# Retention's value projection, two heads in one 512-column pass

## The chip, the cores and the metric

The kernel runs on one core of a Trainium2 chip. The metric is the time of one execution on the device in microseconds. All stages of the kernel run in one launch; weights come from the chip's memory.

## The reference, cut to what matters

Two transformer blocks follow each other on 1024 tokens of width 1024. The part that the change touches is retention in the first block: four heads, with keys and queries of 128 columns and values of 256.

```python
h = rmsnorm(x, pre_mix_norm)
q_r, k_r, v_r, g_r, ... = split(h @ w_in)        # widths 512, 512, 1024, 1024, ...
# per head, chunks n of 128 tokens:
qk      = (q_n @ k_n.T) * decay
o_n     = qk @ v_n + (q_n * qdec) @ s            # v_n: 128 x 256
s       = gamma**128 * s + (k_n * kdec).T @ v_n
ret     = silu(g_r) * groupnorm(o)
```

The rest of the two blocks (attention, gates, two large feed-forward parts) is the same in both kernels.

## The kernel before, in words

Every engine runs its own program, and the five programs are written from the same generators, so that each engine meets the pieces of work in the same order; what an engine needs from another it waits for on a semaphore. TensorE (PE) multiplies, ScalarE (ACT) and VectorE (DVE) empty PSUM and do the elementwise work, GpSimd (POOL) some of it, and SyncE (SP) issues the DMAs.

A product in full precision is made of three matmuls in a reduced format: each operand is split into a high and a low part, and `mm3` (L659 to L662) adds high x high, high x low and low x high. The split hidden state is `hhi`, `hlo` (features on partitions, tokens along the row). Weights come in pieces of 128 x 1024 numbers. SP fetches a piece into one of three raw buffers (`raw`, L2686) as soon as the low part of the piece three before it has been formed. ACT copies it to its high part (`whi`, L1192) and DVE subtracts (`wlo`, L1757) into one of five slots, once PE is through with the piece five before. This is asked for in program order by `Feed.done` (L152): when a piece is done, the pieces up to five behind it are split there and then on ACT and DVE.

Projections with features on partitions (q, k, the gates) use `half_product` (L664): per piece two halves of 512 tokens, each of 24 matmuls of 512 columns with a `yield` after 12. The value projection has tokens on partitions: `token_product` (L684) makes, for a tile of 128 tokens and one head, 24 matmuls of 256 columns, the hidden state stationary and the weights moving. Per head there are 8 tiles, and two pieces, which stay in their slots until the last tile. ACT copies each tile to `rv` (L1344). `wide_product` (L697) is the same with 512 columns and four pieces; the second block's value projection uses it.

`retention_order` (L360) sets the order. `proj(0)` runs alone. Then, for each head h, the main work (two gate pieces of head h, then q, k and v of head h+1; for head 3 the last three gates) is interleaved with the side work `retention(h)`. `interleave` (L215) gives one side step per `ratio` main steps: 1.2 for heads 0 to 2, 1.0 for head 3. A main step is 12 matmuls of 512 columns or one value tile. The side work has 20 steps: for each of eight chunks a step `rt` (L843, L845: scores and transposed keys) and a step `ro` (L851, L855, L861: output and state update), two empty steps, and two steps `rT` of transposes (L872). On DVE `rt` stands for the masked scores `ss` (L1930) and the scaled queries (L1937), `ro` for the state `rs` (L1943, L1946) and the statistics (L1953, L1955); the first empty step holds the normalisation (L1960), `rT` the product with the gate into `ret` (L1976). On ACT they stand for the scaled keys `kd` (L1374) and the copy of `ro` (L1379). A gate is emptied by ACT (tanh, L1356), POOL (L2564) and DVE (L1911, `rg`). PE waits for `ss` before each `ro`.

The lines that the steps below name: `Feed.ahead` and `done` L140 and L152, `fetch` L2682, `values_evac` L1339, `retention` on PE L834 and on DVE L1919, `lsig` L502, `swahi` L506.

Of the kernel before, what the change touches and what calls it, by code (L numbers as in the profile page):

```python
# [7 lines left out]
F32R = mybir.dt.float32r  # L8
# [5 lines left out]
T = 1024  # L14
D = 1024
NT = 8
# [47 lines left out]
class Tally:  # L64
# [24 lines left out]
    def ok(self, *name):  # L89
        if not self.building:  # L90
            return None, 1
        topic, count = self.value[name]
        return self.sem(topic), count
# [116 lines left out]
def run(gen):  # L210
    for _ in gen:
        pass
# [53 lines left out]
            next(side, None)  # L266


def token_major(feed, token_product, name, col, spec):
    ns = [feed.piece("T", name, col, 0), feed.piece("T", name, col, 4)]  # L270
    for t in range(NT):
        token_product(ns, t, spec)
        if t == 7:
            for n in ns:
                feed.done(n)
        yield


def token_wide(feed, wide_product, name, spec):
    ns = [feed.piece("V", name, k) for k in range(4)]  # L280
    for t in range(NT):
        wide_product(ns, t, spec)
        if t == 7:
            for n in ns:
                feed.done(n)
        yield
# [70 lines left out]
        yield from values(n)  # L357


def retention_order(feed, half_product, token_product, q, k, v, g, lgate, retention, gates_left):  # L360

    def proj(h):
        yield from feature_major(feed, half_product, "q_r", h, q(h))
        yield from feature_major(feed, half_product, "k_r", h, k(h))
        yield from token_major(feed, token_product, "v_r", 256 * h, v(h))

    def main(h):
        for m in range(2):
            yield from feature_major(feed, half_product, "g_r", 2 * h + m, g(h, m))
        if h < 3:  # L370
            yield from proj(h + 1)
        else:
            lgate()
            yield from gates_left()

    run(proj(0))
    for h in range(4):
        interleave(main(h), retention(h), 1.2 if h < 3 else 1.0)


ITEMS = [(t, Q) for t in range(4) for Q in range(2)]
# [55 lines left out]
def programs(nc, ctx, I, out, sg, cd, yd, xd, ud, fd):  # L437
# [9 lines left out]
    def bank_of(*group):  # L447
        return bank[tally.banks[group]]

    def free(*group):  # L450

        return tally.sem(f"free{tally.banks[group]}"), 1

    def at(name, kb, shape, dt=F32):
        return nc.alloc_sbuf_tensor_at(name, shape, dt, offset=base + int(kb * 1024))
# [35 lines left out]
    rq = [at(f"rq{i}", FO + 4 * i, [128, T]) for i in range(2)]  # L491
    rk = [at(f"rk{i}", FO + 8 + 4 * i, [128, T]) for i in range(2)]
    rv = [at(f"rv{i}", FO + 16 + 8 * i, [128, NT, 256]) for i in range(2)]
    rg = at("rg", FO + 32, [128, 2, T])
    ro = at("ro", FO + 40, [128, NT, 256])
    dect = at("dect", FO + 48, [128, 1028])
# [2 lines left out]
    kd = at("kd", FO + 55.03125, [128, 128])  # L499
    rq2 = at("rq2", FO + 72, [128, 128])  # L500
    tb = at("tb", FO + 72.5, [128, 128])
    lsig = [at(f"lsig{i}", FO + o, [128, T]) for i, o in enumerate((0, 8, 16, 20))]  # L502


    rethi = at("rethi", HO, [128, 8, T], F32R)
    swahi = [at(f"swahi{k}", FO + o, [128, T], F32R) for k, o in enumerate((4, 12, 24, 28))]  # L506
    retlo = at("retlo", XO, [128, 8, T], F32R)
    swalo = at("swalo", FO + 56, [128, 4, T], F32R)
    Z = at("Z", HO + 32, [128, 8, T])
# [145 lines left out]
    def tensor_program(e):  # L655
# [25 lines left out]
                feed.done(n)  # L681
            yield

        def token_product(ns, t, spec):  # L684
            group, hi, lo = spec
            P, free = ring.open(*group, t)
            if t == 0:
                e.wait_ge(*ok("wlo", ns[1]))
            if free:
                e.wait_ge(*free)  # L690
            for k in range(8):
                n, c = ns[k // 4], 256 * (k % 4)
                i = mm3(P[:, 0:256], hi[:, k, 128 * t:128 * t + 128], lo[:, k, 128 * t:128 * t + 128],
                        whi[n % SLOTS][:, c:c + 256], wlo[n % SLOTS][:, c:c + 256], k == 0, k == 7)
            i.then_inc(*ring.full(*group, t))

        def wide_product(ns, t, spec):  # L697
            group, hi, lo = spec
            P, free = ring.open(*group, t)
# [134 lines left out]
        def retention(h):  # L834
            i = h % 2
            qtmp = [rq2, tb]
            for n in range(8):
                c = slice(128 * n, 128 * n + 128)
                P, free = ring.open("rt", h, n)
                e.wait_ge(*free)  # L840
                if n == 0:
                    e.wait_ge(*ok("free", "v_r", h, 7))
                x = e.matmul(P[:, 0:128], rk[i][:, c], rq[i][:, c], start=True, stop=True)  # L843
                if n < 7:
                    x = e.transpose(P[:, 128:256], rk[i][:, c], ident[:, :])  # L845
                x.then_inc(*ring.full("rt", h, n))
                yield
                P, free = ring.open("ro", h, n)
                e.wait_ge(*free)
                e.wait_ge(*ok("ss", h, n))  # L850
                x = e.matmul(P[:, 0:256], ss[n % 2][:, :], rv[i][:, n, :], start=True, stop=n == 0)  # L851
                if n > 0:
                    e.wait_ge(*ok("qd", h, n))
                    e.wait_ge(*ok("free", "kv", h, n - 1))
                    x = e.matmul(P[:, 0:256], qtmp[n % 2][:, :], rs[(n - 1) % 2][:, :], start=False, stop=True)  # L855
                x.then_inc(*ring.full("ro", h, n))
                if n < 7:
                    P, free = ring.open("kv", h, n)
                    e.wait_ge(*free)
                    e.wait_ge(*ok("free", "rt", h, n))  # L860
                    e.matmul(P[:, 0:256], kd[:, :], rv[i][:, n, :], start=True, stop=True).then_inc(*ring.full("kv", h, n))  # L861
                yield
            yield
            yield
            for m in range(2):
                for q in range(2):
                    P, free = ring.open("rT", h, m, q)
                    e.wait_ge(*free)
                    if m == 0 and q == 0:
                        e.wait_ge(*ok("rn", h))  # L870
                    for j in range(4):
                        x = e.transpose(P[:, 128 * j:128 * j + 128], ro[:, 4 * q + j, 128 * m:128 * m + 128], ident[:, :])  # L872
                    x.then_inc(*ring.full("rT", h, m, q))
                yield

        retention_order(feed, half_product, token_product,
                        lambda h: (("q_r", h), hhi, hlo, None), lambda h: (("k_r", h), hhi, hlo, None),
                        lambda h: (("v_r", h), hhi, hlo), lambda h, m: (("g_r", h, m), hhi, hlo, None),
                        nothing, retention, lambda: gates(range(13, 16)))
        tally.alias(("retention",), ring.latest)  # L880

# [175 lines left out]
                yield from feature_major(feed, half_product, "k_2", m, (("k_2", m), yhi, ylo, None))  # L1057

        interleave(qk_products(), idle(14), 1.5)
        run(token_wide(feed, wide_product, "v_2", (("v_2",), yhi, ylo)))  # L1060
        tally.alias(("v2_end",), ring.latest)


# [123 lines left out]
    def scalar_program(e):  # L1187
# [148 lines left out]
        interleave(gates(range(13), sig, ("ht", 7)), swa_order(swa_scores, swa_values), 0.95)  # L1336


        def values_evac(h):  # L1339
            def evac(t):  # L1340
                e.wait_ge(*ok("full", "v_r", h, t))
                if t == 0 and h > 1:
                    e.wait_ge(*ok("full", "ro", h - 2, 7))
                e.activation(rv[h % 2][:, t, :], bank_of("v_r", h, t)[:, 0:256], ACT.Copy).then_inc(*free("v_r", h, t))  # L1344
            return evac

        def before(h):
# [320 lines left out]
        first_stack()  # L1668
        e.wait_ge(*ok("qm", 0, 1, 1))
        e.activation(QM[0][1][64:128, :], q2[64:128, 0, :], ACT.Copy).then_inc(*up("qx", 0))  # L1670
        run(token_wide(feed, token_product, "v_2", v2_evac))


        def pooled(g):
# [79 lines left out]
    def vector_program(e):  # L1754
# [621 lines left out]
        for j in range(2):  # L2376
# [4 lines left out]
            e.memset(QM[0][j][o:o + 64, :].bitcast(F32), 0.0).then_inc(*up("aux", 0, j, 1))  # L2381
            e.wait_ge(*ok("aux", 0, j, 1))
            e.memset(QM[0][j][o + 32:o + 34, :].bitcast(F32), 1.0).then_inc(*up("aux", 0, j, 2))
        run(token_wide(feed, token_product, "v_2", v2_low))


        def pooled(g):
# [293 lines left out]
    def sync_program(e):  # L2681
# [281 lines left out]
        e.wait_ge(*ok("cst", 1))  # L2963
        fetch_c(0)
        feed.cap = CAT
        run(token_wide(feed, nothing, "v_2", None))


        def duplicates(t):
# [91 lines left out]
def pack(inputs, descs):  # L3061
# [17 lines left out]
    for n, d in enumerate(descs):  # L3079
        w = cuts[d[1]]  # L3080
        if d[0] == "F":
            wp[n].reshape(128, 8, 128)[:] = w[:, 128 * d[2]:128 * d[2] + 128].reshape(8, 128, 128).transpose(1, 0, 2)
        elif d[0] == "T":
            wp[n].reshape(128, 4, 256)[:] = w[128 * d[3]:128 * d[3] + 512, d[2]:d[2] + 256].reshape(4, 128, 256).transpose(1, 0, 2)
        elif d[0] == "V":
            wp[n].reshape(128, 2, 512)[:] = w[256 * d[2]:256 * d[2] + 256].reshape(2, 128, 512).transpose(1, 0, 2)
        elif d[0] == "B":
            k, c = d[2] // 2, 512 * (d[2] % 2)
            wp[n].reshape(128, 2, 512)[:] = w[512 * d[3]:512 * d[3] + 512, c:c + 512].reshape(2, 2, 128, 512)[:, k].transpose(1, 0, 2)
        elif d[0] == "D":  # L3090
            wp[n] = w[128 * d[2]:128 * d[2] + 128]
        else:
            wp[n].reshape(128, 2, 4, 128)[:] = w[:, 256 * d[2]:256 * d[2] + 256].reshape(4, 128, 2, 128).transpose(1, 2, 0, 3)
# [35 lines left out]
```

## Time and profile before

| | |
|---|---|
| median of 3 runs | 2548.62 us (2547.71 to 2549.22) |
| the profiled execution | 2549.9 us, span 2548.0 us |
| PE busy | 2496.6 us, 98% of the span |
| DVE, ACT, POOL busy | 1510.3, 1069.4, 189.7 us |
| share of the chain that ended last | PE 90%, DVE 6%, ACT 2%, DMA 1% |
| mean granted clock of TensorE | 0.995 |

The span goes from the first to the last instruction of the profiled execution. A row of a timeline gives the start in microseconds from the span's start, the time it took in microseconds, the engine, the line, the operation, output and inputs by the program's names, the shape and the count of merged instructions; in brackets the engine's idle time just before it and what ended it. Durations of matmuls overlap, so the time that a run of them takes is read from the starts. A matmul of full-precision operands appears twice (x2), for its two passes.

### The profile page before, as it was taken

How to read it: one execution, taken by the hardware profiler on the slowest of the kernel's cores; microseconds unless marked ns; L12 is line 12 of the kernel's file. 1: busy time of each engine (PE TensorE's matmuls, PEld its weight loads, DVE VectorE, ACT ScalarE, POOL GpSimd, SP SyncE). 2: the span in 40 equal slices, each digit the busy share in tenths (PEclk: the TensorE clock that was granted, in tenths of full speed). 3: DMA queues.
4: the chain of work that ended last, by engine and by line, in shares of the span. 5: the costliest groups of instructions: out<-in, count | busy, mean ns of one | idle time of the engine just before them, and what ended most of it. 6: DMA issues, size and time to landing. Idle time of an engine off the chain costs nothing.

```text
span 2548.0 us, 30521 instructions
## 1 busy us (share of the span) xinstructions
PE 2496.6 (98%) x11808; PEld 2058.3 (81%) x11808; DVE 1510.3 (59%) x2211; ACT 1069.4 (42%) x1708; POOL 189.7 (7%) x173
## 2 busy tenths in 40 slices
PE   7999999999999999999999999999999999999998
PEld 6777888888888788888888887866787888888886
DVE  4345223223533786877664754358767677876668
ACT  4344322222322564444434543357526544444432
POOL 0000000000020300000000110145111000000000
PEclk9999999999999999999999999999999999999999
DMA  4121211101421466778865541101315577788554
GB/s 166 67 75 66 75 42 37 39 34 57 159 83 64 164 214 209 243 256 330 306 247 182 188 155 62 34 20 40 116 51 194 184 250 262 252 336 323 188 188 168
DMA packets 148304, 390.06 MB, mean 153 GB/s; under 512 B 15136, under 2 KB 15392, under 8 KB 148032
## 3 DMA queue, kind: packets, MB, share of 16 engines
q1 hardware_dynamic: 148160, 388.11, 43.6%
q8 instruction: 94, 1.54, 0.2%
q14 instruction: 50, 0.41, 0.0%
HBM read 284.17 MB, written 100.73 MB: 151 GB/s over the span
## 4 chain that ended last, share of the span: by engine, by line
PE 90%; DVE 6%; ACT 2%; DMA 1%; issue 1%; SPq 0%; POOL 0%; DVEq 0%; ACTq 0%
PE bank L660 28%; PE bank L662 27%; PE bank L661 27%; DVE PAl L2402 1%; PE bank L734 1%; DVE st L2397 1%; DVE wlo L1757 1%; PE bank L784 1%; PE bank L1119 1%; PE bank L851 1%; PE bank L861 0%; PE bank L855 0%; PE bank L819 0%; ACT PAh L1697 0%; ACT whi L1192 0%
## 5 line engine op out<-in xcount | busy, mean ns | idle before, releaser
L1757 DVE TENSOR_TENSOR wlo<-raw,whi 128x1024 fp32r<-128x1024 f32 x122 | 150.1, 1237 | 255.3 <-ACT whi L1192 254.5
L660 PE MATMUL bank<-hhi,whi 128*128 128x512 f32 x608 | 249.0, 409 | 1.7 <-DVE hlo L1782 1.7
L662 PE MATMUL bank<-hhi,wlo 128*128 128x512 f32 x608 | 238.6, 392 | 0.0
L661 PE MATMUL bank<-hlo,whi 128*128 128x512 f32 x608 | 238.3, 392 | 0.0
L1192 ACT ACTIVATE whi<-raw 128x1024 fp32r<-128x1024 f32 x122 | 127.6, 1053 | 113.5 <-PE bank L662 86.2
L1490 ACT ACTIVATE r<-r 128x512 f32<-128x512 f32 x96 | 60.7, 632 | 190.7 <-DVE r L2227 133.1
L660 PEld LDWEIGHTS bank<-hhi,whi 128*128 128x128 f32 x608 | 114.8, 189 | 29.4 <-issue 6.7
L662 PEld LDWEIGHTS bank<-hhi,wlo 128*128 128x128 f32 x608 | 114.6, 188 | 25.3
L661 PEld LDWEIGHTS bank<-hlo,whi 128*128 128x128 f32 x608 | 115.0, 189 | 22.3
L660 PE MATMUL bank<-yhi,whi 128*128 128x512 f32 x192 | 74.9, 390 | 0.0
L662 PE MATMUL bank<-yhi,wlo 128*128 128x512 f32 x192 | 74.7, 389 | 0.0
L661 PE MATMUL bank<-ylo,whi 128*128 128x512 f32 x192 | 74.7, 389 | 0.0
L660 PE MATMUL bank<-whi,hhi 128*128 128x256 f32 x256 | 74.2, 290 | 0.0
L662 PE MATMUL bank<-whi,hlo 128*128 128x256 f32 x256 | 72.4, 283 | 0.0
L661 PE MATMUL bank<-wlo,hhi 128*128 128x256 f32 x256 | 72.4, 283 | 0.0
L660 PE MATMUL bank<-uw0bh,uw0ah 128*128 128x512 f32 x176 | 68.6, 390 | 0.1
L660 PE MATMUL bank<-uw1bh,uw1ah 128*128 128x512 f32 x176 | 68.5, 389 | 0.0
L662 PE MATMUL bank<-uw0bh,uw0al 128*128 128x512 f32 x176 | 68.5, 389 | 0.0
L662 PE MATMUL bank<-uw1bh,uw1al 128*128 128x512 f32 x176 | 68.5, 389 | 0.0
L661 PE MATMUL bank<-uw0bl,uw0ah 128*128 128x512 f32 x176 | 68.5, 389 | 0.0
L661 PE MATMUL bank<-uw1bl,uw1ah 128*128 128x512 f32 x176 | 68.5, 389 | 0.0
L2592 POOL TENSOR_TENSOR accX<-accX,acc 128x1024 f32<-128x1024 f32 x8 | 20.1, 2514 | 597.0 <-DVE acc L2282 597.0
(457 smaller groups left out, 7079.2 us busy)
## 6 DMA issues: line engine op xcount, KB each, us to landing
raw<-wp_d SPq DMA_DIRECT2D x122, 512.0 KB, 3.6
ra<-ud_d SPq DMA_DIRECT2D x112, 512.0 KB, 4.5
rawp<-wp_d SPq DMA_DIRECT2D x32, 1024.0 KB, 5.8
ud_d<-us SPq DMA_DIRECT2D x128, 256.0 KB, 5.7
rbh<-wp_d SPq DMA_DIRECT2D x64, 512.0 KB, 6.1
ud_d<-f SPq DMA_DIRECT2D x96, 256.0 KB, 2.2
rbw<-wp_d SPq DMA_DIRECT2D x48, 512.0 KB, 3.6
rbx<-wp_d SPq DMA_DIRECT2D x32, 512.0 KB, 8.3
```

The source lines that it names most:

```text
L660: e.matmul(P, sh, mh, start=first, stop=False, skip_group_check=more)
L661: e.matmul(P, sh, ml, start=False, stop=False, skip_group_check=more)
L662: return e.matmul(P, sl, mh, start=False, stop=last, skip_group_check=more)
L734: i = e.transpose(P[:, 128 * j:128 * j + 128], src[:, 128 * k:128 * k + 128], ident[:, :])
L784: i = e.matmul(P[:, 256 * (m % 2) + j0:256 * (m % 2) + 256], qs[64 * g:64 * g + 64, m, 128 * n:128 * n + 128], ks[64 * g:64 * g + 64, 128 ...
L851: x = e.matmul(P[:, 0:256], ss[n % 2][:, :], rv[i][:, n, :], start=True, stop=n == 0)
L1119: x = e.transpose(P[:, 128 * ii:128 * ii + 128], Pu[u % 2][ii][:, 128 * k:128 * k + 128], ident[:, :])
L1192: e.activation(whi[n % SLOTS][:, :], raw[n % RAWS][:, :], ACT.Copy).then_inc(*up("whi", n))
L1490: e.activation(r[:, :], r[:, :], ACT.Relu).then_inc(*up("relu", tag, name, p))
L1757: e.tensor_tensor(out=wlo[n % SLOTS][:, :], in0=raw[n % RAWS][:, :], in1=whi[n % SLOTS][:, :].bitcast(F32), op=ALU.subtract).then_inc(*up( ...
L2397: e.tensor_reduce(st[:, m:m + 1], psum[:, b:b + w], AXIS.X, ALU.min).then_inc(*up("mn", u, ii))
L2402: e.tensor_tensor(out=PAl[n % 3][:, c], in0=bank_of("pt", n)[:, c], in1=PAh[n % 3][:, c].bitcast(F32), op=ALU.subtract).then_inc(*free("pt ...
```

## The change

Values of two heads are projected at once. `proj(h)` projects values only for even h, with `token_wide` and `wide_product` (512 columns, four pieces, tiles of two heads), so heads 0 and 1 get theirs before head 0's retention, heads 2 and 3 during head 1's. ACT copies each tile in two activations, to the buffers of the two heads. Head 2's values get a buffer of their own, `rv2`, in the region of the last head's result; head 3's go to head 0's buffer. The ratios of `interleave` become 0.8, 1.2, 0.8 and 1.0, because the main work of heads 0 and 2 has 16 steps now (24 before). Two of the buffers `lsig` and two of `swahi` change places within the freed regions. `token_major` and `token_product` go; `token_wide` takes a column offset.

```diff
-def token_major(feed, token_product, name, col, spec):
-    ns = [feed.piece("T", name, col, 0), feed.piece("T", name, col, 4)]
...
-def token_wide(feed, wide_product, name, spec):
-    ns = [feed.piece("V", name, k) for k in range(4)]
+def token_wide(feed, wide_product, name, col, spec):
+    ns = [feed.piece("V", name, k, col) for k in range(4)]
     for t in range(NT):
         wide_product(ns, t, spec)
         if t == 7:
             for n in ns:
                 feed.done(n)
         yield
...
     def proj(h):
         yield from feature_major(feed, half_product, "q_r", h, q(h))
         yield from feature_major(feed, half_product, "k_r", h, k(h))
-        yield from token_major(feed, token_product, "v_r", 256 * h, v(h))
+        if h % 2 == 0:
+            yield from token_wide(feed, wide_product, "v_r", 256 * h, v(h // 2))
...
-        interleave(main(h), retention(h), 1.2 if h < 3 else 1.0)
+        interleave(main(h), retention(h), (0.8, 1.2, 0.8, 1.0)[h])
...
+    rv2 = at("rv2", XO + 24, [128, NT, 256])
+
+    def rv_of(h):
+        return (rv[0], rv[1], rv2, rv[0])[h]
...
-    lsig = [at(f"lsig{i}", FO + o, [128, T]) for i, o in enumerate((0, 8, 16, 20))]
+    lsig = [at(f"lsig{i}", FO + o, [128, T]) for i, o in enumerate((0, 8, 24, 28))]
...
-    swahi = [at(f"swahi{k}", FO + o, [128, T], F32R) for k, o in enumerate((4, 12, 24, 28))]
+    swahi = [at(f"swahi{k}", FO + o, [128, T], F32R) for k, o in enumerate((4, 12, 16, 20))]
...
                 if n == 0:
-                    e.wait_ge(*ok("free", "v_r", h, 7))
+                    e.wait_ge(*ok("free", "v_r", h // 2, 7))
...
-                x = e.matmul(P[:, 0:256], ss[n % 2][:, :], rv[i][:, n, :], start=True, stop=n == 0)
+                x = e.matmul(P[:, 0:256], ss[n % 2][:, :], rv_of(h)[:, n, :], start=True, stop=n == 0)
...
-        def values_evac(h):
+        def values_evac(p):
             def evac(t):
-                e.wait_ge(*ok("full", "v_r", h, t))
-                if t == 0 and h > 1:
-                    e.wait_ge(*ok("full", "ro", h - 2, 7))
-                e.activation(rv[h % 2][:, t, :], bank_of("v_r", h, t)[:, 0:256], ACT.Copy).then_inc(*free("v_r", h, t))
+                e.wait_ge(*ok("full", "v_r", p, t))
+                if t == 0 and p:
+                    e.wait_ge(*ok("full", "ro", 0, 7))
+                    e.wait_ge(*ok("free", "O", 7, 1))
+                e.activation(rv_of(2 * p)[:, t, :], bank_of("v_r", p, t)[:, 0:256], ACT.Copy)
+                e.activation(rv_of(2 * p + 1)[:, t, :], bank_of("v_r", p, t)[:, 256:512], ACT.Copy).then_inc(*free("v_r", p, t))
             return evac
```

## Rows read from the trace of the kernel before

**Rows 1.** The page: the chain that ended last, shares by engine.
```profile
PE 90%; DVE 6%; ACT 2%; DMA 1%; issue 1%; SPq 0%; POOL 0%; DVEq 0%; ACTq 0%
```
**Rows 2.** Busy time (and instructions) of PE, PEld, DVE, ACT, POOL in the stretch of retention.
```profile
341.67:637.00 295.33, 293.96 (x1633) 256.87 (x1632) 93.79 (x229) 78.82 (x146) 11.76 (x19) 1.00 0.12 41
```
**Rows 3.** Timeline of PE: the first narrow value matmul; first and last of 24 wide ones.
```profile
310.07 0.28 PE L660 MATMUL bank<-whi,hhi 128*128 128x256 f32 x1
...
1634.64 0.39 PE L660 MATMUL bank<-whi,yhi 128*128 128x512 f32 x1
...
1639.85 0.39 PE L662 MATMUL bank<-whi,ylo 128*128 128x512 f32 x1
```
**Rows 4.** Timelines around the end of head 0's value projection, by engine.
```profile
333.11 0.40 PE L660 MATMUL bank<-hhi,whi 128*128 128x512 f32 x1
...
338.58 0.38 PE L843 MATMUL bank<-rq,rk 128*128 128x128 f32 x2
...
341.67 0.60 PE L851 MATMUL bank<-rv,ss 128*128 128x256 f32 x2
...
333.31 0.38 ACT L1344 ACTIVATE rv<-bank 128x256 f32<-128x256 f32 x1 [2.50 <-PE bank L662]
333.59 2.00 ACT L1192 ACTIVATE whi<-raw 128x1024 fp32r<-128x1024 f32 x2
...
334.67 2.36 DVE L1757 TENSOR_TENSOR wlo<-raw,whi 128x1024 fp32r<-128x1024 f32 x2 [21.60 <-ACT whi L1192]
...
335.93 1.46 SPq L2686 DMA_DIRECT2D raw<-wp_d  x2
```
**Rows 5.** Timelines of SP and ACT: fetches out of an idle queue.
```profile
1479.34 1.28 SPq L2686 DMA_DIRECT2D raw<-wp_d  x3
...
1482.77 1.06 ACT L1192 ACTIVATE whi<-raw 128x1024 fp32r<-128x1024 f32 x1 [3.77 <-DMA raw<-wp_d]
1484.79 1.06 ACT L1192 ACTIVATE whi<-raw 128x1024 fp32r<-128x1024 f32 x1 [0.96 <-DMA raw<-wp_d]
```
**Rows 6.** Timelines of DVE and PE: head 0, the second chunk.
```profile
347.44 1.21 DVE L1757 TENSOR_TENSOR wlo<-raw,whi 128x1024 fp32r<-128x1024 f32 x1
348.57 0.28 DVE L1930 TENSOR_TENSOR ss<-bank,dect 128x128 f32<-128x128 f32 x1
...
349.00 0.67 PE L851 MATMUL bank<-rv,ss 128*128 128x256 f32 x2 [0.46 <-DVE ss L1930]
```
**Rows 7.** Timelines of PE and DVE: from head 2 to head 3.
```profile
577.45 1.03 PE L872 MATMUL bank<-ident,ro 128*128 128x128 f32 x8
...
581.29 1.28 DVE L1976 TENSOR_TENSOR ret<-bank,rg 128x512 f32<-128x512 f32 x2
582.49 0.28 DVE L1930 TENSOR_TENSOR ss<-bank,dect 128x128 f32<-128x128 f32 x1
...
584.16 0.60 PE L851 MATMUL bank<-rv,ss 128*128 128x256 f32 x2
```
**Rows 8.** Timelines of PE and DVE: head 3, the third chunk.
```profile
594.94 0.38 PE L843 MATMUL bank<-rq,rk 128*128 128x128 f32 x2
...
598.03 0.60 PE L851 MATMUL bank<-rv,ss 128*128 128x256 f32 x2
...
595.47 0.29 DVE L1930 TENSOR_TENSOR ss<-bank,dect 128x128 f32<-128x128 f32 x1 [0.35 <-PE bank L845]
```
**Rows 9.** Timeline of PE: head 0, the seventh chunk, behind a value tile.
```profile
390.25 0.28 PE L662 MATMUL bank<-whi,hlo 128*128 128x256 f32 x1
390.52 0.67 PE L851 MATMUL bank<-rv,ss 128*128 128x256 f32 x2
```
**Rows 10.** Timeline of PE, then a stretch's busy times, granted clock (0.50), DMA.
```profile
273.65 0.63 PE L819 MATMUL bank<-ident,p 128*128 128x128 f32 x4 [1.80 <-DVE p L1879]
...
1927.65 0.50 PE L660 MATMUL bank<-zhi,whi 128*128 128x512 f32 x1 [3.50 <-DVE wlo L1757]
...
1928.13:1931.55 3.42, 3.42 (x10) 2.62 (x9) 2.27 (x4) 1.37 (x2) 0.90 (x1) 0.50 0.28 104
```

More of the change, by code:

```diff
@@ L266, in feature_major_start @@
             next(side, None)
-def token_major(feed, token_product, name, col, spec):
-    ns = [feed.piece("T", name, col, 0), feed.piece("T", name, col, 4)]
[L271 to L276, printed above, removed]
-def token_wide(feed, wide_product, name, spec):
-    ns = [feed.piece("V", name, k) for k in range(4)]
+def token_wide(feed, wide_product, name, col, spec):
+    ns = [feed.piece("V", name, k, col) for k in range(4)]
     for t in range(NT):
@@ L357, in swa_order, with retention_order @@
         yield from values(n)
-def retention_order(feed, half_product, token_product, q, k, v, g, lgate, retention, gates_left):
+def retention_order(feed, half_product, wide_product, q, k, v, g, lgate, retention, gates_left):
     def proj(h):
@@ L682, in half_product @@
             yield
[L684 to L695, printed above, removed]
         def wide_product(ns, t, spec):
@@ L860, in retention @@
                     e.wait_ge(*ok("free", "rt", h, n))
-                    e.matmul(P[:, 0:256], kd[:, :], rv[i][:, n, :], start=True, stop=True).then_inc(*ring.full("kv", h, n))
+                    e.matmul(P[:, 0:256], kd[:, :], rv_of(h)[:, n, :], start=True, stop=True).then_inc(*ring.full("kv", h, n))
                 yield
@@ L874, in retention @@
                 yield
-        retention_order(feed, half_product, token_product,
+        retention_order(feed, half_product, wide_product,
                         lambda h: (("q_r", h), hhi, hlo, None), lambda h: (("k_r", h), hhi, hlo, None),
-                        lambda h: (("v_r", h), hhi, hlo), lambda h, m: (("g_r", h, m), hhi, hlo, None),
+                        lambda p: (("v_r", p), hhi, hlo), lambda h, m: (("g_r", h, m), hhi, hlo, None),
                         nothing, retention, lambda: gates(range(13, 16)))
@@ L1059, in tensor_program @@
         interleave(qk_products(), idle(14), 1.5)
-        run(token_wide(feed, wide_product, "v_2", (("v_2",), yhi, ylo)))
+        run(token_wide(feed, wide_product, "v_2", 0, (("v_2",), yhi, ylo)))
         tally.alias(("v2_end",), ring.latest)
@@ L1670, in scalar_program @@
         e.activation(QM[0][1][64:128, :], q2[64:128, 0, :], ACT.Copy).then_inc(*up("qx", 0))
-        run(token_wide(feed, token_product, "v_2", v2_evac))
+        run(token_wide(feed, token_product, "v_2", 0, v2_evac))
         def pooled(g):
@@ L2383, in vector_program @@
             e.memset(QM[0][j][o + 32:o + 34, :].bitcast(F32), 1.0).then_inc(*up("aux", 0, j, 2))
-        run(token_wide(feed, token_product, "v_2", v2_low))
+        run(token_wide(feed, token_product, "v_2", 0, v2_low))
         def pooled(g):
@@ L2965, in sync_program @@
         feed.cap = CAT
-        run(token_wide(feed, nothing, "v_2", None))
+        run(token_wide(feed, nothing, "v_2", 0, None))
         def duplicates(t):
@@ L3082, in pack @@
             wp[n].reshape(128, 8, 128)[:] = w[:, 128 * d[2]:128 * d[2] + 128].reshape(8, 128, 128).transpose(1, 0, 2)
-        elif d[0] == "T":
-            wp[n].reshape(128, 4, 256)[:] = w[128 * d[3]:128 * d[3] + 512, d[2]:d[2] + 256].reshape(4, 128, 256).transpose(1, 0, 2)
         elif d[0] == "V":
-            wp[n].reshape(128, 2, 512)[:] = w[256 * d[2]:256 * d[2] + 256].reshape(2, 128, 512).transpose(1, 0, 2)
+            wp[n].reshape(128, 2, 512)[:] = w[256 * d[2]:256 * d[2] + 256, d[3]:d[3] + 512].reshape(2, 128, 512).transpose(1, 0, 2)
         elif d[0] == "B":
```

## The prediction

> **What bounds the kernel now.** I read the chain of waits first: it lies on TensorE (PE) for 90% of the span [rows 1], so a change counts by what it does to PE's own time and by the waits it puts in front of PE. Next the busy time by stretches: in the retention stage PE is busy 293.96 of 295.33 us [rows 2]. There is nearly no idle time to win there, but also any new wait of PE is paid in full. Then the timeline of PE, for the pitch from one matmul's start to the next one's: a printed duration (0.28 us for 256 columns, 0.39 for 512) holds the drain, which overlaps the next matmul, and the durations alone would promise 65 us (768 x 0.28 - 384 x 0.39) where the pitches give 5 [rows 3]. Last the rows of ScalarE (ACT), VectorE (DVE) and the DMA queue around the end of the value projection.
>
> I count from E, the instant at which PE starts what follows the last value tile, and take the profiled execution, 2549.9 us (span 2548.0 and 1.9 around it); it lies 1.3 above the median of the runs, 2548.6.
>
> **1. The width.** 768 matmuls of 256 columns go, 384 of 512 come. The 256-wide pitch is (333.11 - 310.07) / 192 = 0.1200 us, the 512-wide one (1639.85 - 1634.64) / 23 = 0.2265 [rows 3, 4]; the wide run has the form of the new one, hidden values stationary and a 512-wide moving operand. A pair becomes 0.0135 us cheaper: 384 x 0.0135 = **-5.2 us**. The bounds are the two rows' rounding, -4.7 to -5.6.
> The Trainium skill, page TensorE: Matmul & The Clock Gate, section Back-to-back issue gap, gives a warm gap of N/2.4 ns plus about 2.5 ns. By that a pair would save only 2.5 ns and the change 1.0 us instead of 5.2; this trace shows some 13 ns a matmul beyond its columns, at both widths, and the measurement decides.
>
> **2. The end of a wide projection.** This is the term that turns the sign. Four weight pieces instead of two are released together, after tile 7, and each release makes ACT form the high part of one more piece (`whi`) and DVE its low part (`wlo`). In the trace two are formed: the copy of tile 7 at E+0.20, `whi` at E+0.48 and 0.95 later, `wlo` 1.08 after its `whi`, the next 1.14 after that, and the queue sends for a new raw piece 0.04 us after the first `wlo` ends [rows 4]. With the change the tile's copy is two activations (0.28 more), so `whi` starts at E+0.76 and the three pieces whose raw data are there have `wlo` at 1.84, 2.98 and 4.12. The fourth has no raw data: there are three raw buffers, and its fetch waits for the first `wlo`, which ends at 3.06. Fetch to `whi` takes 3.43 us (1482.77 - 1479.34) [rows 5], so `whi` is at 6.53 and `wlo` at 7.61.
> Queued behind this fourth `wlo` on DVE is the first masked score block `ss` of the next head, and behind that stands PE, at the head's first `ro` product. After a projection without rest, as at head 0: `ss` 1.13 after the `wlo` starts and PE 0.43 after `ss` starts [rows 6], so PE goes on at E+9.17. It gets there by itself, with one main step (12 matmuls of a gate product) ahead of `rt0` and one behind (the new ratio), at 2.74 (half of 338.58 - 333.11) + 3.09 (341.67 - 338.58, `rt0` and a step) = E+5.83 [rows 4]. Wait: **3.3 us**. At head 2 the two `ret` products of head 1 stand between (1.20 us to `ss`), so PE goes on at 7.61 + 1.14 + 1.20 + 0.43 = E+10.38; head 3 of the trace has this very order, and there PE arrives at 584.16 - 577.45 = E+6.71 [rows 7]. Wait: **3.7 us**. In the trace neither place waits, since two pieces end 2.4 us earlier and need no fetch. Bounds: the same fetch for nothing late (the third rival below, 2.3 us for both) and a `whi` 5.1 us after the fetch, as for the second of the fetches issued together (1484.79) [rows 5], 10.3 for both; I take 7.0, the row of a first fetch out of an idle queue, which this one is.
>
> **3. The rhythm of heads 0 and 2.** These heads' main work loses the value tiles: 16 steps of 2.72 us for 20 retention steps, at ratio 0.8. Every fifth retention step follows the one before at once. Written out, the order doubles `rt2 ro2`, `ro4 rt5`, `rt7 ro7` and the last two transposes. `ro` after `rt` without a main step between waits for `ss`: `ss` starts 0.53 after `rt2` and PE could go on 0.43 later, at 0.96, where now `rt` itself costs 3.09 - 2.72 = 0.37 [rows 8, 6]. That is 0.59; for `rt7`, which lacks the transpose, I take the same; four times: **+2.3 us** (0.3 each at least, as `ss` needs `rt`'s end and its own 0.29 us; 0.8 at most with a late DVE). The wait of 0.62 at `ro1` (0.46 printed as idle and 0.16 behind the drain of the matmul before, 0.39 - 0.23) [rows 6], where a gate's product with `rg` and a `wlo` are ahead of `ss`, exists in heads 0 to 2. With one main step ahead of `rt1`, as in head 3, it goes in heads 0 and 2, but the same neighbours (the end of the second gate piece, `rt4`, one step of `q`, `ro4`) bring it back at `ro4`: 0. In head 1 it stays. A 0.15 us wait at `ro6` behind a value tile (0.27 for 0.12) [rows 9] goes three times: **-0.4**. The transposes need the normalised `ro`; its chain over ACT and DVE begins with the empty step and has two main steps, 5.4 us, to run in, where it had more: 0, at most +0.4.
>
> **4. At nothing.** Copies out of PSUM: 32 either way. Pieces: eight either way, so SP issues as many fetches; in this stage nothing else stands in its queue until the last gates, and POOL is not moved past. The fourth piece at the start of a wide projection is split when `q` is done; the 10.9 us of `k` cover it, and without them it would cost the 2.3 us of a `whi` and a `wlo`. The moved regions (`rv2`, `lsig`, `swahi`) wait for events tens of us back.
>
> Sum without the clock: -5.2 + 7.0 + 2.3 - 0.4 = **+3.7 us**.
>
> **5. The clock.** An idle time of 3.50 us before PE is followed by 3.42 us at half the granted clock (1.2 instead of 2.4 GHz); that costs half of it, 1.7 us; an idle time of 1.80 is followed by none [rows 10]. My two waits, as the trace would print them (0.16 less, for the drain), are 3.2 and 3.5 us: nearest to the first row, a little under it. Bounds 0 and 3.4 us; I take one of the two, **+1.7**. So 2549.9 + 3.7 + 1.7 = 2555.3, and 1.3 less on the median's scale: **2554.0 us**.
>
> **The rivals.**
> - *Both waits, clock held*: +3.7, 2552.3 us. For it: both waits lie under 3.50. Against it: by little.
> - *Both waits, clock halved twice*: +7.1, 2555.7. For it: the second wait equals the row that is followed by the slow clock.
> - *On the other side, the fourth piece is in time*: if its raw data are there 3.6 us after E, its `wlo` follows the third at 5.26. PE then goes on at 5.26 + 1.13 + 0.43 = E+6.82 and E+8.03, two waits of 1.0 and 1.3 with no clock loss: 2548.6 - 5.2 + 2.3 + 1.9 = 2547.6, not slower. For it: fetches in this stage normally go out tens of us ahead. Against it: three raw buffers and the order of the splits.
> - *Faster*: neither the splits nor the doubled steps reach PE: -5.2 - 0.4, 2543.0. Against it: both waits are program order on DVE and not a matter of speed.
> - *The width saves nothing much*: the change does not do what it says, because the 13 ns a matmul beyond its columns (0.1200 us against 256/2.4 ns, 0.2265 against 512/2.4) are a matter of the neighbours and not of the count. With 0 instead of -5.2 the forecast becomes 2559.2. Against it: the two long runs [rows 3]. The Trainium skill's page named in step 1 stands near this rival, and the trace does not agree with it.
> - *One more wait of some 3 us*, for instance a late piece ahead of the wide tiles: 2557.
>
> **How the numbers follow.** Forecast (one clock loss) 0.35, none 0.25, two 0.20, fourth piece in time 0.08, faster 0.04, no gain from the width 0.03, another wait 0.05. A measurement of this kernel can tell about 0.2%, 5.1 us, so the lines are 2543.5 and 2553.7. The forecast lies just behind the upper line; with about 1 us of spread in its terms I give two thirds of it to slower. Slower: two thirds of 0.35, nearly all of 0.20, 0.08, and a little of 0.25, together 0.54. Faster 0.04. The rest, 0.42, is the same. The range, 2550.0 to 2557.5, takes the three clock cases with their unknown terms (four doubled steps at 0.3, a landing a little late) and leaves out the two lower rivals (0.12) and the upper ends (about 0.06).
>
> **What the changed profile would show.** Right: value copies 5.44 us apart in the two projections; behind each a fourth `whi` some 6.5 us after E that waited for a DMA; PE's first `ro` product of heads 0 and 2 with 3 to 4 us idle before it, released by `ss`; 0.4 us idle at `ro2`, `ro4`, `ro7` of these heads; the granted clock at 0.5 for one 3.4 us stretch behind at least one of the two. Wrong: PE's idle before these `ro` products under 1.5 us, or a pitch of the wide tiles off 0.227 us, or a span that moves elsewhere than between 310 and 640 us.

## The result, and the profile after

The changed kernel takes 2555.6 us (median; 2552.4 to 2557.5) where the kernel before takes 2548.8 on the same chip: ratio 1.0026 [1.0016, 1.0036], slower by 6.8 us. Two more comparisons on another occasion gave 1.0029 [1.0020, 1.0038] and 1.0028 [1.0019, 1.0037]. The forecast was 2554.0 with 2550.0 to 2557.5 around it and "slower" as the likeliest sign; the nearest of its cases, by the number, is the one with two clock losses, 2555.7. One execution of the kernel before took 3751 us at a mean clock of 0.624 and is left out of all comparisons.

The profiled execution took 2552.65 us, with a span of 2550.9. First the chain that ended last, on the page, against [rows 1]:

```profile
PE 91%; DVE 6%; ACT 2%; issue 1%; DMA 1%; SPq 0%; POOL 0%; DVEq 0%; ACTq 0%
```

Shares of a whole span can't show 7 us. The stretch of the stage can; it is compared with [rows 2]. The other lines are the two long waits of PE and the 3.4 us behind each (columns: busy time and instructions of PE, PEld, DVE, ACT, POOL, then granted clock, DMA share, GB/s):

```profile
341.00:637.00 296.00, 285.76 (x1316) 236.78 (x1315) 95.28 (x231) 76.88 (x144) 11.76 (x19) 0.99 0.13 43
357.60:361.02 3.42, 0.00 (x1) 0.04 (x1) 1.52 (x2) 1.17 (x2) 0.00 (x0) 1.00 0.92 293
361.02:364.44 3.42, 3.42 (x15) 2.85 (x16) 1.54 (x4) 1.09 (x3) 0.62 (x1) 1.00 0.46 163
523.50:526.53 3.03, 0.00 (x1) 0.00 (x0) 2.25 (x3) 0.75 (x1) 0.00 (x0) 1.00 0.68 246
526.53:529.94 3.41, 2.89 (x7) 2.37 (x8) 0.38 (x2) 2.52 (x4) 0.62 (x1) 0.50 0.45 157
```

PE had 1.4 us without work in this stage before; now it has 10.2 (296.00 - 285.76), although it has less to do. The list of waits from 300 to 640 us names what it waits for (total, times, longest), in the kernel before and then in the changed one:

```profile
PE bank L851 <- DVE ss L1930: 1.4, 3, 0.5
```
```profile
PE bank L834 <- DVE ss L1915: 10.2, 9, 3.5
```

Nine waits for the masked scores in place of three: seven of 0.46 to 0.48 us and two of some 3.5. The timelines of PE, DVE, ACT and SP at the first long one (L1742 is the `wlo` of the forecast, L1175 its `whi`, L1915 `ss`):

```profile
308.11 0.39 PE L656 MATMUL bank<-whi,hhi 128*128 128x512 f32 x1
...
350.95 0.39 PE L656 MATMUL bank<-whi,hhi 128*128 128x512 f32 x1
...
351.63 0.39 PE L656 MATMUL bank<-hhi,whi 128*128 128x512 f32 x1
...
361.02 0.67 PE L834 MATMUL bank<-rv,ss 128*128 128x256 f32 x2 [3.42 <-DVE ss L1915]
...
353.46 3.50 DVE L1742 TENSOR_TENSOR wlo<-raw,whi 128x1024 fp32r<-128x1024 f32 x3 [42.35 <-ACT whi L1175]
359.32 1.23 DVE L1742 TENSOR_TENSOR wlo<-raw,whi 128x1024 fp32r<-128x1024 f32 x1 [2.36 <-ACT whi L1175]
360.58 0.29 DVE L1915 TENSOR_TENSOR ss<-bank,dect 128x128 f32<-128x128 f32 x1
...
358.23 1.06 ACT L1175 ACTIVATE whi<-raw 128x1024 fp32r<-128x1024 f32 x1 [2.91 <-DMA raw<-wp_d]
...
354.72 6.18 SPq L2671 DMA_DIRECT2D raw<-wp_d  x4
```

Read it from the bottom. SP sends for the fourth raw piece at 354.72, when the first of the three `wlo` is done; the data let ACT start `whi` at 358.23, 3.51 us later; DVE, idle for 2.36 us, forms `wlo` at 359.32, and only then, at 360.58, the `ss` that PE has wanted since 357.60. Nothing here is slow. DVE stands idle with `ss` next but one in its program.

The second place has the `ret` products between `wlo` and `ss`:

```profile
516.62 1.04 PE L855 MATMUL bank<-ident,ro 128*128 128x128 f32 x8
...
527.05 1.19 PE L834 MATMUL bank<-rv,ss 128*128 128x256 f32 x2 [3.55 <-DVE ss L1915]
...
523.19 1.06 ACT L1175 ACTIVATE whi<-raw 128x1024 fp32r<-128x1024 f32 x1 [2.87 <-DMA raw<-wp_d]
...
524.28 1.22 DVE L1742 TENSOR_TENSOR wlo<-raw,whi 128x1024 fp32r<-128x1024 f32 x1 [2.33 <-ACT whi L1175]
525.43 1.28 DVE L1961 TENSOR_TENSOR ret<-bank,rg 128x512 f32<-128x512 f32 x2
526.62 0.28 DVE L1915 TENSOR_TENSOR ss<-bank,dect 128x128 f32<-128x128 f32 x1
```

### The profile page after: what moved, and what is told of

Same layout as the page of the kernel before. It is cut to its first block, busy times and chain, and to the rows that moved or that the text cites. A ratio compares the mean times of both kernels' runs of the same rounds, so it can differ in the third digit from the quotient of the medians.

```text
span 2550.9 us, 29750 instructions
## 1 busy us (share of the span) xinstructions
PE 2492.7 (98%) x11424; PEld 2039.3 (80%) x11424; DVE 1510.1 (59%) x2211; ACT 1067.3 (42%) x1708; POOL 190.5 (7%) x173
## 4 chain that ended last, share of the span: by engine, by line
PE 91%; DVE 6%; ACT 2%; issue 1%; DMA 1%; SPq 0%; POOL 0%; DVEq 0%; ACTq 0%
PE bank L656 28%; PE bank L658 28%; PE bank L657 28%; DVE PAl L2387 1%; PE bank L717 1%; DVE wlo L1742 1%; DVE st L2382 1%; PE bank L834 1%; PE bank L767 1%; PE bank L1102 1%; PE bank L844 0%; PE bank L838 0%; PE bank L802 0%; ACT whi L1175 0%; ACT PAh L1682 0%
## 5 line engine op out<-in xcount | busy, mean ns | idle before, releaser
L1742 DVE TENSOR_TENSOR wlo<-raw,whi 128x1024 fp32r<-128x1024 f32 x122 | 150.2, 1238 | 275.5 <-ACT whi L1175 274.5
L1175 ACT ACTIVATE whi<-raw 128x1024 fp32r<-128x1024 f32 x122 | 127.7, 1054 | 120.0 <-PE bank L658 86.2
L656 PE MATMUL bank<-uw2bh,uw2ah 128*128 128x512 f32 x160 | 62.2, 389 | 0.0
L657 PE MATMUL bank<-uw2bl,uw2ah 128*128 128x512 f32 x160 | 62.2, 389 | 0.0
L658 PE MATMUL bank<-uw2bh,uw2al 128*128 128x512 f32 x160 | 62.2, 389 | 0.0
```

The costliest lines, as they stand in the source:

```text
L656: e.matmul(P, sh, mh, start=first, stop=False, skip_group_check=more)
L657: e.matmul(P, sh, ml, start=False, stop=False, skip_group_check=more)
L658: return e.matmul(P, sl, mh, start=False, stop=last, skip_group_check=more)
L1175: e.activation(whi[n % SLOTS][:, :], raw[n % RAWS][:, :], ACT.Copy).then_inc(*up("whi", n))
L1742: e.tensor_tensor(out=wlo[n % SLOTS][:, :], in0=raw[n % RAWS][:, :], in1=whi[n % SLOTS][:, :].bitcast(F32), op=ALU.subtract).then_inc(*up( ...
```

## The experiments

Seven runs were made in two groups, each group on one chip beside the kernel before. Two yardsticks serve for all. The first is the **length of the stage** in the profiled execution, from the first value matmul to the start of the last transposes of head 3, less what the lower clock cost it: half of PE's busy time in each stretch at 0.5 (as the 2.89 in the last row above; what of a stretch falls on an idle PE costs nothing):

| kernel | from | to | length | cost of the clock | without it |
|---|---|---|---|---|---|
| before | 310.07 | 646.42 | 336.35 | 0 | 336.35 |
| changed | 308.11 | 650.72 | 342.61 | 1.4 | 341.2 |
| e1_three | 309.78 | 643.93 | 334.15 | 0 | 334.15 |
| e2_steps | 309.37 | 650.61 | 341.24 | 4.4 | 336.9 |
| e3_all | 308.87 | 637.76 | 328.89 | 0 | 328.89 |
| e4_fill | 309.63 | 650.92 | 341.29 | 0 | 341.29 |
| e5_narrow | 309.04 | 658.36 | 349.32 | 3.3 | 346.0 |

The changed kernel was profiled twice more, in the two control runs below: its stage is 342.56 us long in both, 341.0 and 340.9 without the clock. Of the other kernels there is one profiled execution each.

The second yardstick is the **mean time of all runs**, with (1 - clock) x time beside it, where the clock is the mean granted clock that comes with every run (with their standard errors). As a stretch at 0.5 loses half its length, the product would be what the lower clock cost a run, if PE were busy in all of it and the record of the clock were whole. The record isn't whole. Around 22 us into the span PE's matmuls of 512 columns start 0.43 us apart, about twice their pitch at the full clock. In the kernel before that falls in a stretch at 0.50; in all three profiled executions of the changed kernel the clock reads 1.00 there. The changed kernel, then the one before:

```profile
21.92 0.63 PE L657 MATMUL bank<-hlo,whi 128*128 128x512 f32 x1
22.34 0.63 PE L658 MATMUL bank<-hhi,wlo 128*128 128x512 f32 x1
16.00:24.50 8.50, 6.42 (x23) 5.00 (x22) 6.68 (x10) 6.82 (x14) 0.00 (x0) 1.00 0.78 308
```
```profile
22.96 0.63 PE L661 MATMUL bank<-hlo,whi 128*128 128x512 f32 x1
23.39 0.63 PE L662 MATMUL bank<-hhi,wlo 128*128 128x512 f32 x1
16.67:26.91 10.24, 7.94 (x27) 6.21 (x26) 8.42 (x13) 7.29 (x14) 0.00 (x0) 0.50 0.61 238
```

The product also holds stretches behind the stage, which the change doesn't touch and which come and go: those near 1705 and 1930 us (3.4 us at 0.5 each) stand in the profiles of before, changed, ctrl_after2 and e5_narrow, the second alone in e2_steps, and neither in ctrl_after, e1_three, e3_all and e4_fill. And among the 47 runs of the kernel before the time rises by only 0.41 us for each us of the product. So the product tells a direction; sizes are taken from the mean times. The clock is given to 0.001, 2.5 us, so only means over many runs are of use:

| kernel | runs | median us | mean us | (1 - clock) x time |
|---|---|---|---|---|
| before (both groups) | 47 | 2548.4 | 2547.82 ± 0.3 | 9.4 ± 0.5 |
| changed (both controls) | 22 | 2555.7 | 2555.36 ± 0.5 | 13.5 ± 0.9 |
| e1_three | 11 | 2544.1 | 2544.12 ± 0.5 | 9.0 ± 0.7 |
| e2_steps | 11 | 2549.9 | 2549.32 ± 1.0 | 11.6 ± 1.6 |
| e3_all | 6 | 2539.8 | 2540.17 ± 0.5 | 8.0 ± 1.4 |
| e4_fill | 11 | 2552.3 | 2552.28 ± 0.4 | 10.2 ± 0.7 |
| e5_narrow | 5 | 2562.3 | 2562.78 ± 0.7 | 14.9 ± 1.0 |

**ctrl_after and ctrl_after2: the changed kernel again.** No edit.

> The changed kernel again, beside the others. All theories: 2555.6 us against 2548.8 of the kernel before (ratio 1.0027). The theory of the two waits: PE idle 3.4 and 3.6 us before the first `ro` product of heads 0 and 2, both released by `ss`, as in the first profile; the granted clock halved for 3.4 us behind one or both of them (the first profile had it behind one), so that two executions can differ by 1.7 us. A rival that puts the loss into the wide matmuls themselves expects a pitch above 0.227 us in their runs.

> The changed kernel once more, beside the two that follow: 2555.8 us (2550 to 2559), +7 us on the kernel before.

2555.85 and 2555.57 us. Of the 7.5 us between the means over both groups (2555.36 - 2547.82) the stage without the clock makes 4.8 (341.2 - 336.35). The other 2.7 are left for the clock, wherever in the program it was lost; the product rises too, from 9.4 to 13.5.

**e1_three: the fourth piece is released later.** After tile 7 three pieces are released, the fourth in the middle of the next head's q product, behind several retention steps.

```diff
-            self.ahead(min(n + SLOTS + 1, self.cur + depth))
+            self.ahead(min(n + SLOTS + 1, self.cur + depth) - self.behind)
...
+        if half and name == "q_r" and feed.behind:
+            feed.behind = 0
+            feed.ahead(n + SLOTS)
...
         if t == 7:
+            feed.behind = 1 if name == "v_r" else 0
```

> Only three of the four pieces are released after tile 7, the fourth at the middle of the next q product, so no split has to wait for its fetch; all else as in the changed kernel. Theory (the fetch of the fourth piece holds DVE, and through `ss` PE): both waits go (3.6 and 3.7 us, down to 0 and 0.2), the clock losses behind them too (1.7 to 3.4), so 2555.6 - 7.1 - 2.6 = about 2546. Rival A (it is the number of splits that DVE has to do, 1.14 us each): each wait shrinks by 1.1 us only, the clock may hold, so 2551 to 2553. Rival B (the loss sits elsewhere): 2555.

2544.08 us, ratio to before 0.9984 [0.9975, 0.9993]: 11.8 us under its control, 1.9 under what was expected, and now faster than before. DVE and PE at the first `ro` of head 0, then the list of PE's waits from 300 to 640 us:

```profile
355.13 3.50 DVE L1746 TENSOR_TENSOR wlo<-raw,whi 128x1024 fp32r<-128x1024 f32 x3 [42.35 <-ACT whi L1179]
358.66 0.29 DVE L1919 TENSOR_TENSOR ss<-bank,dect 128x128 f32<-128x128 f32 x1
...
359.10 0.67 PE L838 MATMUL bank<-rv,ss 128*128 128x256 f32 x2
```
```profile
PE bank L838 <- DVE ss L1919: 3.3, 7, 0.5
```

The same three `wlo`, then `ss` at once, and no idle time in front of `ro`; of the nine waits the seven short ones are left. The stage without the clock is 7.0 us shorter (341.2 - 334.15), nearly the two waits. The rest of the 11.8 is left for the clock: the product falls from 13.5 to 9.0, and in this profile the granted clock is 1.00 in the whole stage. So the fourth piece costs more than the two waits alone, and e4_fill takes the second price by itself.

**e2_steps: no doubled steps.** The order of heads 0 and 2 is written out so that the doubled steps are a `ro` and the next `rt`, never an `rt` and its own `ro`; PE gets a wait for k's copies at the first `rt`, which the old order implied.

```diff
+COUNTS = (1, 1, 1, 1, 1, 2, 2, 1, 1, 2, 2, 1, 1, 1, 1, 1)
...
-        interleave(main(h), retention(h), (0.8, 1.2, 0.8, 1.0)[h])
+        if h % 2:
+            interleave(main(h), retention(h), (0.8, 1.2, 0.8, 1.0)[h])
+        else:
+            interleave_by(main(h), retention(h), COUNTS)
...
+                    e.wait_ge(*ok("free", "k_r", h, 1))
```

> Heads 0 and 2 keep 16 main and 20 retention steps, but the doubled steps are now all a `ro` followed by the next `rt`, never an `rt` followed by its own `ro`; the four pieces are released as in the changed kernel. PE also waits explicitly for the copy of k at a head's first `rt`. Theory: the 0.6 us at `ro2`, `ro4` and `ro7` of heads 0 and 2 go, 6 x 0.62 = 3.7 us, the two long waits stay (3.4 and 3.6 us of idle): 2551.9. Rival (the doubling itself is what costs, since the chain of a chunk has 3.6 us less main work to hide behind): as many waits at other places, 2555.

2549.87 us (2543.8 to 2554.3), 6.0 under its control and 2.0 under what was expected; 1.0006 [0.9997, 1.0015], not to be told from before. The list of waits, and the stretches at the lower clock:

```profile
PE bank L851 <- DVE ss L1932: 7.6, 3, 3.6
```
```profile
361.30:368.20 6.90, 5.74 (x14) 4.54 (x15) 2.53 (x6) 1.24 (x3) 0.62 (x1) 0.51 0.35 123
528.60:532.00 3.40, 2.99 (x7) 2.48 (x8) 0.36 (x3) 2.52 (x4) 0.62 (x1) 0.50 0.40 146
```

The six short waits of heads 0 and 2 are gone; the two long ones and head 1's short one are left. The stage without the clock is 4.3 us shorter (341.2 - 336.9); six waits of 0.47 with the 0.16 behind a drain make 3.8 of it, and the rest I did not trace to rows. Nor is the other 1.7 of the 6.0 accounted for: this profile has more of the lower clock in the stage than the changed kernel's (4.4 against 1.4). The scatter goes with the clock: the two runs with a mean clock of 0.998 took 2543.8 and 2544.3 us, the four with 0.993 took 2551.9 to 2554.3.

**e3_all: both edits**, and head 1 at a ratio of 1.0 as head 3 has it.

> Both edits (three pieces, steps in a good order), and head 1 at one retention step per main step, which puts its `ret` products well ahead of the end of the wide projection and removes the 0.62 us at its `ro1`. Theory: only the width is left of the change, and the three old waits at `ro1` and at `ro6` are gone: 2548.8 - 5.2 - 0.4 - 1.9 = 2541.3, faster than both kernels, PE waiting for `ss` nowhere by more than 0.2 us. Rival (the pitches do not add up to a gain): not under 2546.

2539.75 us, ratio 0.9971 [0.9959, 0.9982]: 8.3 us under the kernel before and 16.1 under the changed one, and 1.6 under what was expected. The stretch of the stage:

```profile
300.00:640.00 340.00, 340.00 (x1578) 283.82 (x1577) 108.09 (x253) 92.13 (x170) 13.59 (x22) 1.00 0.13 44
```

PE is busy throughout, and the list of its waits is empty. The parts add: 7.0 (three pieces), 4.3 (steps) and 0.6 for head 1's wait make 11.9; the stage is 12.3 shorter (341.2 - 328.89). This is the version to keep; it beats both.

**e4_fill: the waits stay, PE isn't idle in them.** Twenty matmuls whose result nothing uses stand ahead of PE's wait for `ss` at the first `ro` of heads 0 and 2.

```diff
+                if n == 0 and h % 2 == 0:
+                    for _ in range(20):
+                        e.matmul(P[:, 256:512], hhi[:, 0, 0:128], hhi[:, 0, 0:256], start=True, stop=True)
```

> Twenty matmuls of 256 columns, whose result nothing uses, stand on PE ahead of its wait for `ss` at the first `ro` of heads 0 and 2: 20 x 0.120 = 2.4 us of work in two waits of 3.4 to 3.6 us, so that the wait stays as long as it was and only 1.0 to 1.2 us of it is idle. Theory (the idle time has a second price, 3.4 us at the 1.2 GHz level behind it, 1.7 us each time, in one or both of the two places): the granted clock is 1.0 behind both waits in the profile, the median falls by 1.7 to 3.4 to 2552.4 to 2554.1 us, and the runs lie closer together than those of the changed kernel. Rival (the clock has no part in the retention stage, the waits themselves are longer than the forecast had them): 2555.8, nothing moves; if the added matmuls ran past the end of the wait, above that.

2552.30 us, 3.3 under its control (3.2 ± 0.7 between the means, 2555.45 and 2552.28), just below the expected 2552.4 to 2554.1; the runs lie between 2550.5 and 2554.2 (the control: 2552.3 to 2558.8). PE at head 2, the list of its waits, and the clock behind the two long ones, at head 0 and at head 2:

```profile
524.88 2.55 PE L835 MATMUL bank<-hhi 128*128 128x256 f32 x20
528.52 0.70 PE L837 MATMUL bank<-rv,ss 128*128 128x256 f32 x2 [1.09 <-DVE ss L1918]
```
```profile
PE bank L837 <- DVE ss L1918: 5.3, 9, 1.1
```
```profile
361.50:364.90 3.40, 2.46 (x12) 1.97 (x12) 1.75 (x4) 1.14 (x3) 0.62 (x1) 1.00 0.75 280
527.43:530.83 3.40, 2.31 (x11) 1.88 (x11) 1.03 (x3) 2.30 (x4) 0.00 (x0) 1.00 0.56 190
```

The stage is as long as the changed kernel's without the clock (341.3 against 341.2), and the granted clock is 1.0 behind both waits. `ss` comes as late as before; only PE's idle time ahead of it is shorter, and the kernel is 3.2 us faster. So the idle time has a second price. A loss of 3.4 us would be two stretches at the lower clock, one behind each wait. That it is two isn't shown: each of the three profiled executions of the changed kernel has one in the stage, and e4_fill's profile also lacks the two stretches near 1705 and 1930 us, so a part of the 3.2 may lie behind the stage.

**e5_narrow: the width alone undone.** The two-head value projection in two passes of 256 columns over each tile.

```diff
+            for o in (0, 256) if group[0] == "v_r" else ():
+                for k in range(8):
+                    n, c = ns[k // 2], 512 * (k % 2) + o
+                    i = mm3(P[:, o:o + 256], hi[:, k, 128 * t:128 * t + 128], lo[:, k, 128 * t:128 * t + 128],
+                            whi[n % SLOTS][:, c:c + 256], wlo[n % SLOTS][:, c:c + 256], k == 0, k == 7)
```

> The two-head value projection in two passes of 256 columns over each tile, all else as in the changed kernel: 384 matmuls of 512 columns become 768 of 256. Theory (what a matmul takes beyond its columns is a matter of their count, 13 ns each by the pitches 0.1200 and 0.2265): the pitch in both value projections is 0.120 us and the time rises by 5.2 to 2561.0 us. Rival (2.5 ns each, the Trainium skill's page TensorE: Matmul & The Clock Gate, section Back-to-back issue gap): +1.0, 2556.8. The waits at the first `ro` of heads 0 and 2 stay 3.3 to 3.6 us, as they belong to the feed.

2562.31 us, 6.7 over its control and 1.3 over what was expected. The timeline of PE, from the first matmul of the first value projection to the first of the product behind it:

```profile
309.04 0.28 PE L656 MATMUL bank<-whi,hhi 128*128 128x256 f32 x1
...
355.11 0.40 PE L656 MATMUL bank<-hhi,whi 128*128 128x512 f32 x1
```

384 matmuls in 46.07 us, 0.1200 each. The stage without the clock is 4.8 us longer (346.0 - 341.2), near the 5.1 to 5.2 of the pitches. The other 1.9 of the 6.7 is what this profile loses more to the clock in the stage (3.3 against 1.4); with one execution of each, that is a hint and no more. The two long waits are as they were (3.40 and 3.54). The Trainium skill, page TensorE: Matmul & The Clock Gate, section Back-to-back issue gap, gives N/2.4 + 2.5 ns, for a single matmul by itself; an estimate from it, 384 x 2.5 ns, would be 1.0 us. The measurement does not agree with it, at either width.

## Why the prediction was right, step by step

- **1, the width: right.** 189 matmuls lie between the starts 308.11 and 350.95: 0.2267 us each, so a pair saves 0.0133 and the change 5.1 us (forecast 5.2), and e5_narrow gives 4.8 back. (The rounding of the two rows makes bounds of 5.0 to 5.4; the forecast's were wider.) The rival in which the width saves nothing falls.
- **2, the end of the wide projection: right, and to a tenth or two.** With E at 351.63: fourth `whi` at E+6.60 (forecast 6.53), its `wlo` at 7.69 (7.61), PE on at 9.39 (9.17). PE was through with what it could do at 357.44, the printed 357.60 less the drain: E+5.81 (5.83). The wait is 3.6 us (3.3). At head 2, E at 516.62: `whi` at 6.57, `wlo` at 7.66, PE on at 10.43 (10.38), there at 6.72 (6.71), wait 3.7 (3.7). Together 7.3 for 7.0. Why the fourth piece and not the projection is the cause, e1_three shows: with three pieces released both waits go. Whether DVE's order alone would do, with `ss` ahead of the fourth `wlo`, wasn't tried.
- **3, the rhythm: right in place, a little low.** The three short waits of heads 0 and 2 stand at `ro2`, `ro4` and `ro7`, 0.46 to 0.48 each, and the one of head 1 stays. The stage without the clock is 4.8 us longer than before (341.2 - 336.35); with 5.1 saved and 7.3 waited, 2.6 are left for the rhythm, and e1_three gives 2.9 (334.15 - 336.35 + 5.1), where 2.3 - 0.4 = 1.9 was forecast. What makes the other 0.7 to 1.0 was not traced to rows.
- **4, nothing: no run speaks against it.** No other wait of PE appears in the stage, so the rival of one more late piece falls as well.
- **5, the clock: the term that was too small, and a guess.** I took one loss of the two, +1.7, because both waits lay just under the one row that I had. That row is a matter of chance itself: PE is idle for 3.50 to 3.53 us at its place in all nine profiled executions, and 3.4 us at 0.5 follow in five of them (before, changed, ctrl_after2, e2_steps, e5_narrow) and not in the other four. In the stage the changed kernel's three profiles show one loss each, 1.4 to 1.7 us. The times of many runs say more: 2.7 ± 0.6 (7.5 - 4.8), and by e4_fill 3.2 ± 0.7. That is nearer to two losses than to one, but how many there are in the stage, and how much is lost behind it, stays open. The profiled execution alone would have misled: its 2552.65 lies 3 us under the median.
- **The sum.** Without the clock the forecast was +3.7, and the profiled executions have +4.8. So the waits (0.3), the rhythm (0.7) and the clock (1.0 to 1.5) all came out dearer than forecast, and nothing cancelled. That the time lies on the rival "clock halved twice", 2555.7, is in part luck: that rival added 3.4 to 3.7, and the runs have some 3 on 4.8.
- **A sign named as wrong did show.** The profiled execution moved outside 310 to 640 us too: the first value matmul starts 2.0 us earlier than before (308.11 against 310.07), and 1900.2 us follow the start of the last transposes in place of 1901.6. So the span grew by 2.9 us where the stage grew by 6.3. The work there is the same, and executions of the changed kernel differ by as much among themselves (1900.2, 1897.8 and 1902.2 us behind that point), so this does not count against the mechanism. But one profiled execution against another can't settle a change of some 5 us.
- **The fourth piece in time** and **faster** did not happen, but both can be made: e1_three and e3_all are what the width brings when the splits and the steps don't reach PE.

## What to carry to other kernels

When a wider product holds more weight pieces to its last tile, count the pieces that it releases at once against the raw buffers: the first one beyond them costs a whole fetch, and on an engine that works in program order everything queued behind its split waits too. Hold that piece back by a few steps. When side steps are spread over fewer main steps, double the ones that don't depend on each other. And a wait of TensorE can have its length as one price and the clock behind it as another, which one profile may not show: compare the times of many runs with the wait filled and unfilled, and trust a mean clock only where the matmuls' pitch agrees with it.

## What was not expected of the hardware

The lower clock does not follow from the length of the idle time alone, at these lengths. In three profiled executions of the changed kernel 3.42, 3.29 and 3.15 us without work at head 0 were followed by none, 3.55, 3.46 and 3.49 at head 2 each by 3.4 us at 0.5 (1.2 instead of 2.4 GHz); in e5_narrow 3.40 at head 0 was followed by it; in e2_steps 3.60 was followed by 6.9 us, the double. Nor does the slow stretch begin with the work: here it began at 526.53, 3.03 us into the idle time and 0.52 before PE went on, so that a part of it fell on a PE without work; in [rows 10] it began 0.48 us after PE had gone on. What decides it was not settled. With matmuls in the same waits the profile of e4_fill shows 1.0 in both places.
